# Projection, norm and router in one stage by token tiles; attention pairs and experts written out; tokens fetched as rows

## The reference

```python
x = x + mix                       # mix ends in (...) @ w_o
h = rms_norm(x, norm_ffn_g[i])    # x * rsqrt(mean(x*x) + eps) * g
aff = softmax(h @ w_router)       # 512 tokens x 16 experts
gates, idx = top_k(aff.T, 64)     # each expert takes its 64 best tokens
xe = h[idx]                       # 16 x 64 x 1024
hid = silu(xe @ w_gate) * (xe @ w_up)
x = x + scatter_add(idx, (hid @ w_down) * gates)
```

## Time and profile before

| | |
|---|---|
| median of 3 runs | 2227.78 us (2227.05 to 2231.99) |
| profiled execution: time | 2235.93 us |
| profiled execution: span, first to last instruction | 2234.2 us |
| mean granted TensorE clock | 0.947 of full |
| TensorE matmul busy | 1975.7 us, 88% |
| VectorE, ScalarE, GpSimd busy | 862.1, 509.9, 191.1 us |
| DMA | 450.00 MB, mean 201 GB/s |
| chain that ended last | PE 68%, DMA 12%, DVE 6%, issue 6% |

### The profile page before, as it was taken

One profiled execution on the slowest core, in us unless ns is written; L12 is line 12 of the kernel. 1 busy time (PEld: TensorE's weight loads), 2 busy tenths in 40 slices (PEclk: granted clock), 3 DMA queues, 4 the chain that ended last, 5 costly groups with the idle time before them and its releaser, 6 DMA issues.

```text
span 2234.2 us, 46998 instructions
## 1 busy us (share of the span) xinstructions
PE 1975.7 (88%) x20190; PEld 1103.0 (49%) x20190; DVE 862.1 (39%) x1696; ACT 509.9 (23%) x988; POOL 191.1 (9%) x214
## 2 busy tenths in 40 slices
PE   3689999999998766999999977899996699999998
PEld 2257666766667343444444424566654344444442
DVE  6556565655554124222122211566632422112221
ACT  1133443444343010001111012355521000111100
POOL 0021133113302000000000000111100000000000
PEclk8899999999999877999999998899997799999999
DMA  2111011101100903999999961200050399999996
GB/s 79 32 33 35 9 38 35 40 8 35 39 10 9 381 0 134 429 429 427 429 429 428 428 278 40 106 20 20 20 237 0 137 429 428 428 429 429 428 428 283
DMA packets 78800, 450.00 MB, mean 201 GB/s; under 512 B 12733, under 2 KB 47162, under 8 KB 54074
## 3 DMA queue, kind: packets, MB, share of 16 engines
q1 hardware_dynamic: 78650, 447.73, 48.8%
HBM read 443.78 MB, written 3.93 MB: 200 GB/s over the span
## 4 chain that ended last, share of the span: by engine, by line
PE 68%; DMA 12%; DVE 6%; issue 6%; ACT 3%; DVEq 2%; ACTq 1%; POOLq 1%; SPq 0%; POOL 0%; PEldq 0%; another core or an unknown queue 0%
PE banks L1395 17%; DMA arena<-in_moe_w_down 11%; PE bank L597 7%; PE banks L1380 5%; PE banks L764 4%; PE banks L1246 4%; PE bank L1441 3%; PE bank L1395 3%; PE banks L868 2%; PE banks L1441 2%; PE banks L1783 2%; PE banks L454 1%; PE banks L951 1%; PE banks L1656 1%; PE banks L888 1%
## 5 line engine op out<-in xcount | busy, mean ns | idle before, releaser
L1395 PE MATMUL banks<-arena 128*64 128x512 f32 x2560 | 559.9, 594 | 1.1 <-ACT arena L1447 1.1
L1395 PEld LDWEIGHTS banks<-arena 128*64 128x64 f32 x2560 | 180.0, 137 | 355.2 <-issue 355.2
L597 PE MATMUL bank<-arena 128*128 128x512 f32 x384 | 192.1, 628 | 9.1 <-ACT arena L637 8.4
L1492 DVE TENSOR_TENSOR arena<-arena,bank 128x512 f32<-128x512 f32 x80 | 55.0, 687 | 367.3 <-PE bank L1441 367.3
L1099 POOL TENSOR_TENSOR arena<-arena 128x512 f32<-128x512 f32 x80 | 101.5, 1292 | 438.5 <-DVE arena L1154 438.5
L764 PE MATMUL banks<-arena 64*64 64x64 f32 x5632 | 126.3, 221 | 9.9 <-issue 6.4
L764 PEld LDWEIGHTS banks<-arena 64*64 64x64 f32 x5632 | 110.5, 134 | 48.4 <-issue 39.2
L1380 PE MATMUL banks<-arena 128*128 128x128 f32 x1024 | 123.5, 283 | 9.6 <-DVEq L347 9.6
L1380 PEld LDWEIGHTS banks<-arena 128*128 128x128 f32 x1024 | 120.4, 198 | 21.2 <-issue 11.4
L1395 PE MATMUL bank<-arena 128*64 128x512 f32 x512 | 115.5, 595 | 12.7 <-DMA arena<-in_moe_w_down 12.6
L1453 ACT ACTIVATE arena<-banks 128x512 f32<-128x512 f32 x32 | 19.1, 597 | 417.6 <-PE banks L1395 417.6
(11 more groups left out here) (297 smaller groups left out, 2617.9 us busy)
## 6 DMA issues: line engine op xcount, KB each, us to landing
arena<-in_moe_w_gate SPq DMA_DIRECT2D x64, 2048.0 KB, 21.7
arena<-in_moe_w_up SPq DMA_DIRECT2D x64, 2048.0 KB, 15.7
arena<-in_moe_w_down SPq DMA_DIRECT2D x64, 2048.0 KB, 16.5
arena<-in_x SPq DMA_DIRECT2D x8, 512.0 KB, 11.6
arena<-in_rw_wr SPq DMA_DIRECT2D x8, 512.0 KB, 3.9
arena<-in_rw_wk SPq DMA_DIRECT2D x8, 512.0 KB, 5.9
arena<-in_rw_wv SPq DMA_DIRECT2D x8, 512.0 KB, 6.0
arena<-in_rw_wo SPq DMA_DIRECT2D x1, 4096.0 KB, 18.0
```

Of the source, the lines that this page charges most:

```text
L597: last = nc.tensor.matmul(b[:, :], w_sl[:, n, k, :], xmix[n][:, k, :], start=(k == 0), stop=(k == ND - 1))
L1395: last = nc.tensor.matmul(ps[bank][z * CAP:(z + 1) * CAP, :], st[:, k, :], ring[c % RING][:, k, z * 512:(z + 1) * 512], start=(c % 2 == 0 ...
L1492: nc.vector.tensor_tensor(xs, xs, ps[b][:, :], ALU.add).then_inc(free[b], 1)
```

## The change

It does five things.

1. Projection, norm and router become one stage (`out_pe`, `out_act`, `out_pool`, `out_dve`) that goes by token tiles. While the projection of tile t runs, `x` of tile t-1 is transposed (not the normed `h`), and the router's logits are taken from it: the gain is multiplied into the router's weights (`router_pad`), and the root of each token is multiplied onto the logits afterwards (`route_dve`). The 8 logits matmuls of a tile go to four column strips of 32, and a matmul with `sel` adds the four. Two meetings go. The normed `h` is made beside it: the product with the gain on POOL, the scale on ACT.
2. `h` is stored to DRAM (in the output tensor, as rows), and the tokens of a pair of experts are fetched from there by an indirect DMA from POOL, 128 rows of 4 KB, instead of 32 matmuls. The row numbers come from 4 matmuls of `pick` with the token numbers. 8 transposes replace the gather matmuls.
3. The ring has 8 slots instead of 6. Seven are loaded ahead; the eighth lies in `hT` and is loaded when the logits are done.
4. The expert pairs are written out instead of looped.
5. The 8 attention pairs are written out in one stage with one meeting behind them, and the last one makes no projections for a next pair.

The router's weights are now loaded in another layout (one row of 16 numbers per partition and block), and the gain a second time as columns.

The core of the diff:

```diff
-RING = 6
+RING = 8
...
+        order = []
+        for t in range(NT):
+            order += [(("out", t, z), (2 * t + z) % 4) for z in range(2)]
+            order += [(("tr", t, i), 4 + i) for i in range(2)] + [(("lg", t), 6 + t % 2)]
+        oj = Jobs(order + [("sel", 0), ("at", 1), ("st", 2)])
...
+            def turn_x(t):
+                pe.wait_ge(x_ready, t + 1)
+                for i in range(2):
+                    b = open_job(pe, oj, ("tr", t, i))
+                    for k in range(4):
+                        last = nc.tensor.transpose(b[:, tile(k)], x_sb[:, t, tile(4 * i + k)], ident[:, :])
+                    last.then_inc(full[4 + i], 1)
+            def logits(t):
+                for i in range(2):
+                    job_read(pe, oj, ("tr", t, i))
+                b = open_job(pe, oj, ("lg", t))
+                for k in range(ND):
+                    g = slice(k % 4 * 32, k % 4 * 32 + 32)
+                    last = nc.tensor.matmul(b[g, 0:P], router_pad[:, k, :], hT[:, k, tile(t)], start=(k < 4), stop=(k >= 4),
+                                            skip_group_check=True)
+                last.then_inc(full[6 + t % 2], 1)
...
+            out(0, 0)
+            out(0, 1)
+            pe.wait_ge(router_ready, 1)
+            for t in range(1, NT):
+                out(t, 0)
+                turn_x(t - 1)
+                out(t, 1)
+                logits(t - 1)
+            turn_x(NT - 1)
+            for t in range(NT - 1):
+                select(t)
+            logits(NT - 1)
+            select(NT - 1)
+            pe.wait_ge(aff_ready, 1)
+            b = open_job(pe, oj, "at")
             for t in range(NT):
-                for z in range(2):
-                    b = open_job(pe, oj, (t, z))
-                    for k in range(ND):
-                        last = nc.tensor.matmul(b[:, :], yT[:, k, t * P:(t + 1) * P], wo_sb[:, k, z * 512:(z + 1) * 512],
-                                                start=(k == 0), stop=(k == ND - 1))
-                    last.then_inc(full[oj[(t, z)][0]], 1)
...
+            def logits(t):
+                b = job_full(act, oj, ("lg", t))
+                nc.scalar.copy(lgT[:, tile(t)], b[:, 0:P]).then_inc(free[6 + t % 2], 1)
+            square(0)
+            for t in range(1, NT):
+                turned(t - 1)
+                scaled(t - 1)
+                logits(t - 1)
+                square(t)
+            turned(NT - 1)
+            logits(NT - 1)
+            act.wait_ge(logit_ready, 1)
+            nc.scalar.activation(logit, logit, ACT.Exp).then_inc(exp_ready, 1)
+            scaled(NT - 1)
...
+                nc.gpsimd.tensor_tensor(sel, sel, ident[:, 32 * g:32 * g + NE], ALU.add)
+            pool.drain().then_inc(router_ready, 1)
+            pool.wait_ge(ld_gain[2 * layer + 1], 16)
+            for t in range(NT):
+                pool.wait_ge(sq_ready, t + 1)
+                nc.gpsimd.tensor_scalar(ssum[:, t:t + 1], ssum[:, t:t + 1], 1.0 / D, NORM_EPS, ALU.mult, ALU.add)
+                pool.drain()
+                nc.gpsimd.tensor_tensor(rstd4[:, t:t + 1], ssum[:, t:t + 1], mhalf[:, 0:1], ALU.pow).then_inc(rstd_ready, 1)
+                if t == NT - 1:
+                    nc.gpsimd.iota(iota_i, [[1, CAP]], base=0, channel_multiplier=0)
+                    nc.gpsimd.iota(token_i, [[P, NT]], base=0, channel_multiplier=1)
+                    nc.gpsimd.memset(slot[:, :, NE:NE + 2], -1.0)
+                    nc.gpsimd.memset(aff[:, :, NE:NE + 2], 0.0)
+                    pool.drain().then_inc(iota_ready, 1)
+                for h in range(2):
+                    o = slice(h * 512, (h + 1) * 512)
+                    nc.gpsimd.tensor_tensor(h_tok[:, t, o].rearrange("p (k q) -> p q k", k=4), by_row(x_sb[:, t, o]),
+                                            by_row(gain_row[:, o]), ALU.mult)
+                pool.drain().then_inc(h_ready, 1)
...
+            sp.dma_start(router_sb, a["moe_router"][layer].rearrange("(k p) n -> p k n", p=P)).then_inc(ld_router[layer], 16)
+            sp.dma_start(gcol, a["norm_ffn_g"][layer].rearrange("(k p) -> p k", p=P), allow_slow_non_contiguous=True).then_inc(ld_gcol[layer], 16)
...
+        def route_dve(dve, layer):
+            dve.wait_ge(rstd_ready, NT)
+            b = job_full(dve, oj, "sel")
+            dve.sem_inc(hT_read[layer], 1)
+            lg = logit
+            nc.vector.tensor_tensor(lg, b[:, 0:NT * NE].rearrange("p (t e) -> p t e", t=NT), rstd4.unsqueeze(2).to_broadcast([P, NT, NE]), ALU.mult)
...
+        def rows_pe(pe, i):
+            pe.wait_ge(pick_ready, i + 1)
+            b = open_job(pe, xj, ("rows", i))
+            for t in range(NT):
+                last = nc.tensor.matmul(b[:, 0:1], pick[:, t, :], token_f[:, t:t + 1], start=(t == 0), stop=(t == NT - 1))
+            last.then_inc(full[2], 1)
+        def gather_pe(pe, i, layer):
+            pe.wait_ge(ld_rows[layer], 16 * (i + 1))
             for z in range(2):
-                used(pe, z, it, 1)
+                b = open_job(pe, xj, ("x", i, z))
                 for k in range(4):
-                    for t in range(NT):
-                        last = nc.tensor.matmul(ps[z][:, k * P:(k + 1) * P], h_tok[:, t, (4 * z + k) * P:(4 * z + k + 1) * P],
-                                                pick[:, t, :], start=(t == 0), stop=(t == NT - 1))
+                    last = nc.tensor.transpose(b[:, k * P:(k + 1) * P], xe_tok[:, (4 * z + k) * P:(4 * z + k + 1) * P], ident[:, :])
                 last.then_inc(full[z], 1)
...
+        def moe_pool(pool, layer):
+            pool.wait_ge(h_stored[layer], 16 * NT)
+            for i in range(PAIRS):
+                job_read(pool, xj, ("rows", i))
+                if i:
+                    job_full(pool, xj, ("x", i - 1, 1))
+                nc.gpsimd.indirect_dma_start(xe_tok, None, h_dram, bass.IndirectOffsetOnAxis(ap=row_index, axis=0)).then_inc(ld_rows[layer], 16)
...
+            for g in range(RING - 1):
+                load_chunk(sp, layer, g)
+            rows = h_dram.rearrange("(t p) d -> p t d", p=P)
+            for t in range(NT):
+                sp.wait_ge(h_done[layer], t + 1)
+                sp.dma_start(rows[:, t, :], h_tok[:, t, :]).then_inc(h_stored[layer], 16)
+            sp.wait_ge(hT_read[layer], 1)
+            load_chunk(sp, layer, RING - 1)
+            for g in range(RING, CPP * PAIRS):
+                chunk_read(sp, layer, g - RING)
...
+            for u in range(NPAIR):
+                more = u < NPAIR - 1
...
+                out_pool(pool, layer)
+                meet_pool(pool, route_sems)
+                moe_pool(pool, layer)
                 meet_pool(pool, moe_sems, everyone)
```

515 lines of the change are left out of this document (256 added, 259 removed).

## The result

| | before | after |
|---|---|---|
| median of 4 runs each | 2229.69 us (2227.05 to 2231.99) | 2175.93 us (2174.74 to 2179.9) |
| ratio, 95% interval | | 0.9762 (0.9743 to 0.9781) |
| profiled execution: time, span | 2235.93, 2234.2 us | 2174.74, 2172.6 us |
| mean granted TensorE clock | 0.947 | 0.955 |
| TensorE busy | 1975.7 us, 88% | 1872.0 us, 86% |

The change makes the kernel 2.4% faster, 53.8 us between the medians. The forecast was 2171.0 us in a range of 2150 to 2208.

A forecast was written before the change was run, and what follows sets the result against it. Experts were taken to end with the DMA's chunks left after the first used one. Terms -46.9 + 5.0 - 19.6 + 17.5 + 1.2 - 13.6 = -56.4 us; 2235.9 became 2179.5, less 8.1 for the median: 2171 us (2150 to 2208).

The forecast's parts named there:

- The ring: Weight chunks ahead of each layer's experts: eight there at the start instead of six, -19.6 us over both layers.
- The stage: Projection to first expert matmul: -24.2 us in layer 0 and -22.7 in layer 1, together -46.9 us.
- Cold start: First expert chunk of each layer, with TensorE at its low clock: +2.5 us per layer, +5.0 in all (0 to 7).
- Rows by DMA: Seven gathers per layer in the full DMA queue, 1.25 us each: +17.5 us (ends 0 and 4.0 each).
- Written-out code: Instruction fetches of the experts, no longer looped: 0.6 MB more to move, +1.2 us.
- Attention: Layer 1's attention: 8.7 us from three inner meetings gone, 4.9 from the unread last projection, together -13.6 us (-9 to -17).
- lies 8.1 below it: Step from profiled execution to median of the runs: median taken 8.1 us lower, turning 2179.5 into 2171 us.
- A: Rival, expert stretches: each gather holds the DMA stream for its whole 4.0 us, +38.5 us, 2210 us; chance 0.10.
- B: Rival, expert stretches: the gather uses few of the 16 DMA engines, +200 on one engine, 2428 us; chance 0.04.
- C: Rival, experts: TensorE idles between chunks and its clock falls, slower by hundreds of us if it stayed so; chance 0.03.
- D: Rival, projection stage: not hidden between matmuls, TensorE waits 2 us at six hand-overs per layer, +24, 2195 us; chance 0.05.
- E: Rival, experts and attention: the gathers cost nothing and attention gains 17 us, 2150 us; chance 0.04.

## Why the prediction was right, point by point

**What bounds.** Right: the experts end with the bytes behind the first used chunk. The ring was worth 9.8 and 10.1 us per layer for the 9.8 of the sum. One of the signs named is a little off: from the first bytes behind the first used chunk (in the microsecond from 851) to the last (in that from 1294) it is some 443 us, not 439, at 425 GB/s with the gathers in it.

**The stage.** -24.2 and -22.7 were forecast, -25.6 and -24.1 measured. The projection took 62.3 us (64.4 forecast): eight transposes cost 0.87 and not 1.2 us, eight logit matmuls 0.57 and not 1.0, so the four column strips do run side by side (1.8 us would be eight matmuls one after the other). The forecast's own term is off by a little: 3 x 1.2 + 2 x 1.0 is 5.6, not 5.5. The chain behind it was 4.6 us (4.9), the first gather 10.5 (10.0). GpSimd's products were laid under the routing at no cost, and cost 0.9 us per layer. The norm off the chain is 13.5 us of the 49.7 of both stages; the order of TensorE gives some 3. The rest, the two meetings, the rolled passes over four tiles and the cold router matmuls, was not taken apart.

**Cold start.** 2.5 us per layer were forecast; the first 96 records took 22.14 us instead of 20.82, so 1.3: a term that was mis-sized.

**Rows by DMA.** 1.25 us each were forecast, 1.28 and 1.23 (1.30 with the clock allowed for) measured, by taking away and by adding. The two ends of the range, 0 and 4.0, are both out. The cover held: no wait of TensorE for a row DMA but at the first of a layer.

**Written-out code.** 0.23 MB of instructions moved in the window of one layer; 0.6 MB were forecast for both (a fifth of the rate of the earlier trace rows over both stretches is 0.52). Its price was not measured, since no run rolls the experts up again. What there is room for: without gathers in the stream the stretch is 441.35 us, and that of the kernel before, 449.4, less two chunks (9.78), is 439.6; of the 1.7 between them 1.3 are the cold start, so at most some 0.4 per layer are left, where 0.6 were forecast.

**Attention.** -13.6 forecast, -13.2 measured, and +13.3 when put back; but the shares were wrong. The step that failed is "without the three inner meetings the first falls to 25.8 and the second from 27.0": the rows showed intervals around a meeting inside a rolled loop, and I laid the whole of them to the meeting. A bare meeting costs 1.0 us at most (3.1/3); the loop, with a meeting that clears semaphores and waits for SP, adds 2.5 per pass (7.4/3), by a longer idle and the lower clock behind it; and the unread pair costs 2.8 instead of 4.9. The 8.7 forecast for the meetings stand against 10.5 for meetings and loop together, 1.8 too little, and the unread pair was put 2.1 too high: that the total was met is luck.

**The sum and its base.** The sum was -56.4, the two profiles differ by 61.2. The forecast of 2171 still came out 4.9 us too low, because the step "lies 8.1 below it" failed: it took from the forecast what lay between one profiled execution and the median. The changed kernel's profiled execution lies 1.2 below its median, not 8.1 above. The RWKV part alone moved by up to 6 us between profiled executions of the same code. The two errors, 4.8 and 9.3, had opposite signs, and a rounding of 0.4 makes up the rest; so the total came closer than its parts by luck. Counted by medians the gain is 53.8 us and not 61.2: the kernel before ran at 2225 to 2238 us in the comparisons, and its one profiled execution (2235.9) lies near the slow end. In which of its stages those microseconds lie, one profile can't tell.

**Rivals.** A (4.0 us per gather) fell with the doubled gathers: 17.2 us for 14, not 56. B and C did not come: 425 GB/s with the gathers in the stream, clock 1.00. D did not come: no idle time between TensorE's groups in the projection. E had the gathers wrong, and its attention gain of 17 too.

## What to carry to other kernels

Where two resources are nearly in balance, moving work from one to the other is a loss as soon as the receiver is what ends last; price it by what the receiver's stretch grows per piece, and try the version with everything else but that move. In this kernel 9% less work on TensorE per pair (52.4 for 57.5 us) cost 16 us, inside a change that won 54. An interval around a meeting in a rolled loop holds the loop's price too: take it apart before you lay it to either. And work that is "hidden" on an idle engine can still slow an instruction beside it (0.9 us here): compare that instruction's own time before and after.

## What the runs showed of the hardware

- A GpSimd gather of 0.52 MB into a full queue landed 10.9 us after its issue but cost the stream only 1.2 to 1.3 us; in an idle queue the first one of layer 0 was waited for 4.6 us. Time to landing is no price.
- SP stood still for 8.5 to 9.5 us at one issue, whichever request came behind the router's load, while 4 MB of w_o and 2 MB of x were under way; in the kernel before no issue there took over 3.74 us. The router's load in 64-byte runs is what differs ahead of it, but no run takes that away. What counts is which request meets it and who waits behind.
- Behind a TensorE idle of 1.94 us the granted clock fell (0.65 over the next 4 us, 0.50 at its lowest), behind one of 1.28 us it stayed at 1.00, with the same matmuls around it. The rolled loop also loaded ScalarE's table in each pass (1.28 us, hidden), where the written-out code loaded it once.
- A 128x64 VectorE subtraction with two operands in SBUF took 1.10 to 1.12 us while GpSimd multiplied 128x512 tiles, and 0.22 to 0.23 when GpSimd had finished (13 kernels, both layers).
